# First layer's gate and up projections: seven block products in place of eight, for 19 of 22 tile pairs

## What is computed

```python
def swiglu(h, w_gate_up, w_down):
    gate, up = jnp.split(h @ w_gate_up, 2, axis=-1)
    return (jax.nn.silu(gate) * up) @ w_down
...
fx = rms_norm(x, g_ffn[i]) * (1.0 + sc2) + sh2
x = x + ga2 * swiglu(fx, w_gate_up[i], w_down[i])
if update_ctx:
    fc = rms_norm(ctx, g_ffn[i]) * (1.0 + csc2) + csh2
    ctx = ctx + cga2 * swiglu(fc, w_gate_up[i], w_down[i])
```

## Time and profile before

| what | us |
|---|---|
| median of 3 runs (1548.73 to 1551.69) | 1550.38 |
| the profiled execution's own time | 1552.32 |
| its span | 1550.5 |
| PE busy | 1377.4 |
| DVE busy | 699.2 |
| ACT busy | 512.4 |
| POOL busy | 66.2 |

### The profile page before, as it was taken

How to read it: one execution, slowest core, us unless ns; L and a number is a source line. 1 busy time by engine, 2 the same in 40 slices (tenths; PEclk the granted TensorE clock), 3 DMA queues, 4 the chain that set the end, 5 groups by cost and what they waited for, 6 DMA issues and landing times.

```text
span 1550.5 us, 24550 instructions
## 1 busy us (share of the span) xinstructions
PE 1377.4 (89%) x10275; PEld 1043.0 (67%) x10275; DVE 699.2 (45%) x1272; ACT 512.4 (33%) x946; POOL 66.2 (4%) x74
## 2 busy tenths in 40 slices
PE   6999999999999999999999999999987766766664
PEld 3765677887878787757999999899754334333332
DVE  4336546765645444675655657676521011010101
ACT  4426434222122223654444444555411101000001
POOL 1040020000000001111000000000000000000000
PEclk9999999999999999999999999999998878778888
DMA  8990325545844343616665459247899999999996
GB/s 339 411 296 1 136 82 211 200 152 186 299 167 169 114 162 107 207 38 248 212 208 187 130 183 303 84 138 273 360 425 426 425 427 425 426 426 426 426 426 265
DMA packets 159932, 392.40 MB, mean 253 GB/s; under 512 B 11573, under 2 KB 124745, under 8 KB 126026
## 3 DMA queue, kind: packets, MB, share of 16 engines
q1 hardware_dynamic: 159242, 389.34, 66.1%
q10 hardware_dynamic: 576, 1.44, 0.3%
HBM read 389.71 MB, written 1.05 MB: 252 GB/s over the span
## 4 chain that ended last, share of the span: by engine, by line
PE 65%; DMA 24%; DVE 5%; ACT 4%; issue 2%; SPq 0%; DVEq 0%; ACTq 0%
DMA R<-in_w_dram 22%; PE ps L1071 15%; PE ps L1072 15%; PE ps L1079 15%; PE ps L3121 3%; PE ps L1122 2%; PE ps L670 2%; PE ps L1116 2%; PE ps L1117 2%; DMA R<-in_w_ada_dram 2%; PE ps L1572 1%; PE ps L1549 1%; PE ps L3171 1%; PE ps L1517 1%; PE ps L1636 1%
## 5 line engine op out<-in xcount | busy, mean ns | idle before, releaser
L1039 DVE TENSOR_TENSOR WL<-R,WH 128x1024 fp32r<-128x1024 f32 (+1 forms) x201 | 225.2, 1137 | 165.0 <-ACT WH L1029 164.9
L3121 PE MATMUL ps<-R,XG 128*32 128x256 f32 x2048 | 172.8, 497 | 118.4 <-DMA R<-in_w_dram 112.3
L1071 PE MATMUL ps<-HH,WH 128*128 128x256 f32 (+2 forms) x872 | 273.0, 333 | 0.0
L1072 PE MATMUL ps<-HL,WH 128*128 128x256 f32 (+2 forms) x872 | 270.0, 331 | 0.0
L1029 ACT ACTIVATE WH<-R 128x1024 fp32r<-128x1024 f32 (+1 forms) x201 | 190.0, 961 | 140.5 <-PE ps L1079 105.5
L3121 PEld LDWEIGHTS ps<-R,XG 128*32 128x32 f32 x2048 | 87.6, 137 | 197.6 <-issue 179.9
L1071 PEld LDWEIGHTS ps<-HH,WH 128*128 128x128 f32 (+1 forms) x872 | 164.7, 189 | 25.5 <-issue 8.6
L1072 PEld LDWEIGHTS ps<-HL,WH 128*128 128x128 f32 (+1 forms) x872 | 164.1, 188 | 16.5
L1079 PE MATMUL ps<-HH,WL 128*128 128x256 f32 (+2 forms) x872 | 164.9, 331 | 0.0
L1071 PE MATMUL ps<-GH,WH 128*128 128x512 f32 (+1 forms) x480 | 154.5, 340 | 1.4 <-ACT WH L1029 1.4
L1072 PE MATMUL ps<-GL,WH 128*128 128x512 f32 (+1 forms) x480 | 153.4, 339 | 0.0
(11 more groups left out here) (509 smaller groups left out, 1729.1 us busy)
## 6 DMA issues: line engine op xcount, KB each, us to landing
R<-in_w_dram SPq DMA_DIRECT2D x192, 1024.0 KB, 26.5
R<-in_w_ada_dram SPq DMA_DIRECT2D x72, 1024.0 KB, 7.5
R<-in_w_gate_up_dram SPq DMA_DIRECT2D x40, 1024.0 KB, 6.4
R<-in_w_in_dram SPq DMA_DIRECT2D x20, 1024.0 KB, 7.7
R<-in_w_down_dram SPq DMA_DIRECT2D x16, 768.0 KB, 4.3
R<-in_w_down_dram SPq DMA_DIRECT2D x16, 640.0 KB, 4.2
R<-in_w_in_dram SPq DMA_DIRECT2D x8, 512.0 KB, 7.3
R<-in_w_out_dram SPq DMA_DIRECT2D x16, 256.0 KB, 8.3
```

Of the source, the lines that this page charges most:

```text
L1039: last = e.tensor_tensor(L, w, H.bitcast(F32), ALU.subtract)
L1071: e.matmul(b[0:n, 0:N], H[:, k, 0:n], xh(k, N), start=(begins and k == ks[0]), stop=False)
L1072: e.matmul(b[0:n, 0:N], H[:, k, 0:n], xl(k, N), start=False, stop=False)
L3121: mm = e.matmul(PS[4][32 * g:32 * g + 32, 0:256], x[:, 4 * hf + k, :], w[g // 2][:, k, 256 * (g % 2):256 * (g % 2) + 256], start=(hf == 0 ...
```

## The change

- Pairs m = 3 to 10 of half 0 and all 11 of half 1 (numbered p = 0 to 18) are no longer two tiles of 512 columns. The pair's weights are a 2 x 2 arrangement of blocks (gate or up, inputs 0 to 511 or 512 to 1023), the activations another (those inputs, `x` or `ctx`). Seven products of blocks (q = 0 to 6), each 12 matmuls of 256 columns, replace eight. The first three pairs of half 0 (`PLAIN`) stay.
- Three products take a weight block as it is loaded, four take sums of blocks (`SUMS`) which POOL makes: four instructions over 128 x 512 for a pair (`pool_seven`), and a fifth over 128 x 256 that adds two partial results of the pair before (`pool_up`). The activations' sums are made once, by DVE, behind the norm (`dve_sums_of_x`: 8 additions of 128 x 1024, four splits).
- ACT and DVE split each of the seven blocks (128 x 512) by itself, into four buffers in turn; the block that is split at step n is n + 4. DVE adds four partial results of 128 x 256 a pair, ACT copies two. The product with Silu is done for both streams by one DVE instruction.
- Five of the ring's ten slots are held from the start of half 0 to the end of half 1 (`kept`): three for the activations' sums, two for the weights' sums.
- Part 5 of the mixed-in sums has one vector in place of two. The mixed-in work follows product q = 2 of a pair, and the hooks of PE and ACT stand at pairs in place of tiles. One semaphore is renamed at the kernel's end.

Cut to what the prediction speaks of (`act_high_of_x`, `dve_low_of_x` split the activations' sums; `act_block` and `dve_block_low` for the first two blocks of a half are hung on the tile before it):

```diff
-VECTORS_OF = {5: (0, 1), 6: (2,), 7: (2,)}
+VECTORS_OF = {5: (0,), 6: (2,), 7: (2,)}
+PLAIN = 3
+PAIRS = [(half, m) for half in range(2) for m in range(11) if half or m >= PLAIN]
+BLOCKS = 7
...
+                    if i == 0 and (half, c // 128 + j) in PAIRS:
+                        pair_loads.append((gate, up, 128 * j, n))
+                        gate.used = up.used = (s_bl, blocks_split(BLOCKS * len(pair_loads)))
+                        continue
...
+                    if i == 0:
+                        kept = [ring.plan(None, hold=True, parts=0) for _ in range(5)]
...
+            if i == 0 and half:
+                for load in kept:
+                    load.used = (s_bm, BLOCKS * len(PAIRS))
+                    ring.held.discard(load.slot)
...
+    SUMS = [[at(f"SW{y}{q}", [128, 4, 128], F32, slot_at(kept[3 + y].slot) + 2 * KB * q) for q in range(4)] for y in range(2)]
...
+    UT = [TMP[7], TMP[6]]
...
+    def banks(p):
+        r = g00 % 4
+        A, B, C = ((PS[4], PS[5], PS[(r + 2) % 4]), (PS[(r + 3) % 4], PS[r], PS[(r + 1) % 4]))[p % 2]
+        return A[:, 0:256], C[:, 0:256], B[:, 0:256], C[:, 256:512]
...
+    def block_source(n):
+        p, q = divmod(n, BLOCKS)
+        gate, up, col, width = pair_loads[p]
+        if q in (0, 4, 6):
+            load = up if q == 6 else gate
+            k0 = 0 if q == 0 else 4
+            return fm(R[load.slot][:, 0:8 * width], 8)[:, k0:k0 + 4, col:col + 128], (d_ring[load.slot], load.landed)
+        x = {2: 0, 1: 1, 3: 2, 5: 3}[q]
+        return SUMS[p % 2][x][:, :, :], (s_sw, summed_weights(p, x))
+    def act_block(e, n):
...
+        if n >= 4:
+            e.wait_ge(s_bm, n - 3)
+        src, ready = block_source(n)
+        e.wait_ge(*ready)
+        e.activation(BH[n % 4][:, :, :], src, ACT.Copy).then_inc(s_bh, 1)
+    def act_product(e, p, x):
+        e.wait_ge(s_bm, BLOCKS * p + 2 * x + 1)
+        if p >= 2:
+            e.wait_ge(s_gu, number(p - 2) + 1)
+        elif p == 1:
+            e.wait_ge(s_bl, x_split(3))
+        e.activation(UT[p % 2][:, 256 * x:256 * x + 256], banks(p)[2 * x], ACT.Copy).then_inc(s_bh, 1)
+    def dve_block_low(e, n):
+        e.wait_ge(s_bh, high_of[n])
+        src, _ = block_source(n)
+        e.tensor_tensor(BL[n % 4][:, :, :], src, BH[n % 4][:, :, :].bitcast(F32), ALU.subtract).then_inc(s_bl, 1)
...
+    def pool_seven(e):
+        for p in range(len(PAIRS)):
+            gate, up, col, width = pair_loads[p]
+            s1, s2, s3, s4 = (t[:, :, :] for t in SUMS[p % 2])
+            if p == 0:
+                e.wait_ge(*kept[3].after.used)
+            elif p == 1:
+                e.wait_ge(s_bl, x_split(2))
+            else:
+                e.wait_ge(s_bl, blocks_split(BLOCKS * (p - 2) + 6))
+            for load in (gate, up):
+                e.wait_ge(d_ring[load.slot], load.landed)
+            g, u = (fm(R[load.slot][:, 0:8 * width], 8)[:, :, col:col + 128] for load in (gate, up))
+            e.tensor_tensor(s1, u[:, 0:4, :], u[:, 4:8, :], ALU.add).then_inc(s_sw, 1)
+            e.wait_ge(s_sw, summed_weights(p, 0))
+            e.tensor_tensor(s2, s1, g[:, 0:4, :], ALU.subtract).then_inc(s_sw, 1)
+            e.tensor_tensor(s3, g[:, 0:4, :], u[:, 0:4, :], ALU.subtract).then_inc(s_sw, 1)
+            e.wait_ge(s_sw, summed_weights(p, 1))
+            e.tensor_tensor(s4, g[:, 4:8, :], s2, ALU.subtract).then_inc(s_sw, 1)
+            if p and not goes_first(p - 1):
+                pool_up(e, p - 1)
+            if goes_first(p):
+                pool_up(e, p)
+    def pool_up(e, p):
+        ut = UT[p % 2]
+        e.wait_ge(s_cmb, 8 + 4 * p + 2)
+        if p >= 3:
+            e.wait_ge(s_gu, number(p - 3) + 1)
+        e.tensor_tensor(TMP[3 + p % 3][:, 256:512], ut[:, 0:256], ut[:, 256:512], ALU.add).then_inc(s_sw, 1)
...
+    def dve_sums_of_x(e):
+        def whole(k0, c0):
+            return HH[:, k0:k0 + 4, c0:c0 + 256].bitcast(F32), HL[:, k0:k0 + 4, c0:c0 + 256].bitcast(F32)
+        e.wait_ge(*kept[4].after.used)
+        e.wait_ge(s_hl, made(1, 7, 1))
+        for out, k0, c0 in ((F12, 0, 256), (F11, 0, 0), (F22, 4, 256), (F21, 4, 0)):
+            e.tensor_tensor(out[:, :, :], *whole(k0, c0), ALU.add).then_inc(s_cmb, 1)
...
+        for x in range(3):
+            dve_low_of_x(e, x)
...
+    def pe_seven(e, half, after):
+        for p in half_pairs(half):
+            a, b, c, d = banks(p)
+            if p >= 2:
+                e.wait_ge(s_gu, number(p - 2) + 1)
+            if p in half_pairs(half)[0:2]:
+                r, first = g00 % 4, p == half_pairs(half)[0]
+                for x in ((2,) if first else (3, 4, 5)):
+                    t = g00 + x if half == 0 else first_of["down", 0, 0] + x + 2
+                    e.wait_ge(*tiles[t].out)
+            for q, acc in enumerate((a, b, c, d, a, c, d)):
+                n = BLOCKS * p + q
+                xh, xl = x_part(q, False), x_part(q, True)
+                if p == 0 and q in X_READY:
+                    e.wait_ge(s_bl, x_split(X_READY[q] - 1))
+                if q == 3:
+                    e.wait_ge(s_cmb, 8 + 4 * p + 1)
+                elif q == 5:
+                    e.wait_ge(s_cmb, 8 + 4 * p + 2)
+                e.wait_ge(s_bh, high_of[n])
+                for k in range(4):
+                    e.matmul(acc, BH[n % 4][:, k, :], xh(k), start=(q < 4 and k == 0), stop=False, skip_group_check=True)
+                    e.matmul(acc, BH[n % 4][:, k, :], xl(k), start=False, stop=False, skip_group_check=True)
+                e.wait_ge(s_bl, blocks_split(n + 1))
+                for k in range(4):
+                    last = e.matmul(acc, BL[n % 4][:, k, :], xh(k), start=False, stop=(k == 3), skip_group_check=True)
+                last.then_inc(s_bm, 1)
+            after(PAIRS[p][1])
+    def act_rounded(e, p):
+        m, g = PAIRS[p][1], number(p)
+        e.wait_ge(s_gu, g + 1)
+        e.activation(GH[:, m, :], TMP[m % 3][:, :], ACT.Copy).then_inc(s_fh, 1)
+    def act_seven(e, half, then, hook):
+        blocks = half_blocks(half)
+        for x in (2, 3):
+            act_block(e, blocks[x])
+            if half == 0 and x == 2:
+                act_high_of_x(e, 3)
+        for n in blocks:
+            p, q = divmod(n, BLOCKS)
+            m, g = PAIRS[p][1], number(p)
+            T = TMP[m % 3]
+            if q == 0:
+                hook(m)
+            if n + 4 in blocks:
+                act_block(e, n + 4)
+            if q in (0, 2):
+                act_product(e, p, q // 2)
+            if q == 0 and n != blocks[0]:
+                act_rounded(e, p - 1)
+            if n == blocks[-2]:
+                act_split(e, then)
+            if q == 4:
+                e.wait_ge(s_bm, n + 1)
+                e.wait_ge(s_fl, g - 2)
+                e.activation(T[:, 0:256], banks(p)[0], ACT.Silu)
+            elif q == 5:
+                e.wait_ge(s_cmb, 8 + 4 * p + 3)
+                e.activation(T[:, 256:512], T[:, 256:512], ACT.Silu).then_inc(s_silu, 1)
+        act_rounded(e, blocks[-1] // BLOCKS)
...
+    def dve_seven(e, half, then, hook, weigh):
+        blocks = half_blocks(half)
+        for x in (2, 3):
+            dve_block_low(e, blocks[x])
+            if half == 0 and x == 2:
+                dve_low_of_x(e, 3)
+        for n in blocks:
+            p, q = divmod(n, BLOCKS)
+            m, g = PAIRS[p][1], number(p)
+            T, V, ut = TMP[m % 3], TMP[3 + p % 3], UT[p % 2]
+            a, b, c, d = banks(p)
+            if q == 0:
+                hook(m)
+                if n != blocks[0]:
+                    dve_rest(e, p - 1)
+            elif q == 1:
+                e.wait_ge(s_bm, n + 1)
+                dve_pair_sum(e, p, 0, ut[:, 0:256], b)
+            elif q == 3:
+                e.wait_ge(s_bm, n + 1)
+                dve_pair_sum(e, p, 1, ut[:, 256:512], d)
+            elif q == 5:
+                e.wait_ge(s_bm, n + 1)
+                e.wait_ge(s_cmb, 8 + 4 * p + 1)
+                e.wait_ge(s_fl, g - 2)
+                e.tensor_tensor(T[:, 256:512], c, ut[:, 0:256], ALU.add).then_inc(s_cmb, 1)
+            elif q == 6:
+                e.wait_ge(s_bm, n + 1)
+                if p >= 3:
+                    e.wait_ge(s_gu, number(p - 3) + 1)
+                e.tensor_tensor(V[:, 0:256], d, ut[:, 0:256], ALU.add).then_inc(s_cmb, 1)
+                e.wait_ge(s_cmb, 8 + 4 * p + 4)
+                e.wait_ge(s_sw, added(p))
+                e.wait_ge(s_silu, g + 1)
+                e.tensor_tensor(T[:, :], T[:, :], V[:, :], ALU.mult).then_inc(s_gu, 1)
+            if n + 4 in blocks:
+                dve_block_low(e, n + 4)
+            if q == 2:
+                weigh(m)
+        dve_rest(e, blocks[-1] // BLOCKS)
+        dve_split(e, then)
+    def dve_pair_sum(e, p, x, ut, product):
+        e.wait_ge(s_bh, high_of["p", p, x])
+        e.tensor_tensor(ut, product, ut, ALU.add).then_inc(s_cmb, 1)
...
+            if i or half == 0:
```

(34 more changed lines are left out.)

158 lines of the change are left out of this document (128 added, 30 removed).

## The result

| kernel | median us | ratio to before (95%) |
|---|---|---|
| before | 1551.04 (1548.73 to 1552.04, 4 runs) | |
| after | 1683.72 (1683.27 to 1684.77, 4 runs) | 1.0853 (1.0839 to 1.0866) |

The change costs 133 us. The forecast was 1642, with a range up to 1680: the sign and the mechanism of the two halves came as forecast, the size did not, and the stage between the halves was missed. In the profiled executions the span goes from 1550.5 to 1681.5, 131 us more.

What follows compares the result with a forecast made beforehand. The prediction took PE alone to bound the changed stage. Its terms summed to 95.6 us, less 4 for shared effects: 92 on the profiled 1552.3, giving 1644 and a median of 1642, range 1600 to 1680.

Steps and rivals of the forecast that it cites:

- seven dear boundaries: Group boundaries in both halves: late loads, sums and splits in series lose 10.3 us each, 72 in all.
- Rival B: In the halves, POOL and DVE do not hinder each other, ring boundaries remain: cycle 28 to 29, total 1612; chance 0.10.
- D: In the halves, loads do not matter and only POOL and DVE exclusion binds: +24 us, total 1583; chance 0.08.
- The landing of both loads: At a group boundary, gate and up loads land 6.4 us after DVE's split releases their slots.
- The rest of a boundary: After landing: POOL's sums 6.4 us, DVE's product, splits and first partial sum 6.6, the stretch from product 3 13.3.
- the load k = 3: In half 1, this weighting waits a whole landing for a slot freed by the split just ahead: 3 us.
- The start at 5.5: Before the first pair: 2 us from POOL's sums during the norm, 3.5 from ACT's delayed split of tile 5.
- The eighth boundary: Into half 0's last pair: loads of half the size and no sums behind them, 4 us.
- half 1's first pair: At half 1's start, it meets its own sums, the next pair's and part 6's last weighting on POOL: 8 us.
- the small rest: Deductions: 0.9 us for part 5's dropped vector on PE, 4 for overlap with short pairs at half 1's end.
- Rival E: At boundaries, same mechanism but POOL's sums take 2.15 us each and DVE waits longer: 44 more, total 1686; chance 0.13.
- number 3: Sign expected in the profile: DVE's product waits for POOL's short sum, 5 us and more, seven times.

Runs made afterwards that it cites:

- e9: Changed kernel with all five block sums of a pair on DVE instead of POOL, nothing left out: 1635.18 us, ratio 1.0537 to the kernel before.
- e2: Changed kernel with POOL writing constants in place of its five sums per pair: two pairs take 27.4 us, against 36.4 in the changed kernel.
- e1: Changed kernel without gate and up loads after each half's first group, whose weights are reused: two pairs take 26.9 us, against 36.4.
- e6: Changed kernel with SP issuing a group's two weighting loads only after its up load has landed: 1684.34 us, ratio 1.085.
- e8: Changed kernel without part 6's loads and weightings for k from 1 on: first down stage 63.1 us, against 72.7 in the changed kernel.
- e4: Changed kernel with POOL making the previous pair's short sum ahead of the next group's four sums at group boundaries: 1680.51 us, ratio 1.0824.
- e12: Changed kernel without loads and weightings of parts 5 and 7 for k from 1 on: two pairs take 23.9 us, against 36.4.

## Why the prediction was wrong

Right: the one-to-one passing of the stage's loss to the end (131 us in all, 126 of them by the end of half 1), products of 1.44 us on PE, mutual exclusion of POOL and DVE, gate and up released by DVE's splits, seven dear boundaries, PE's waits ahead of products 1 and 3 (4.0 and 6.1 us forecast as 1 to 4 and 5 to 8). The rule of the Trainium skill that the prediction leaned on (SBUF — State Buffer, Who interferes with whom) holds over the whole stage: DVE's product and splits beside POOL's sums took 1.70 and 1.76 us, a split 0.69 in e9, where POOL is quiet, and 0.68 to 0.69 in e2, where POOL only writes. Rival B's cycle of 28 to 29 us was close to the 27.4 that e2 shows for its mechanism, and D's 24 us of exclusion to the 30 of e1 (which also has the length of POOL's sums in it).

Wrong was the size, 92 in place of 131, and these are the terms:

- **The landing of both loads, 6.4**, is 8.0. I took the median over single loads for the time of a pair issued together (e6). 1.6 us at each of seven boundaries.
- **The rest of a boundary.** With the landing a boundary was forecast to lose 10.3 us (a cycle of 32.7) and loses 14.0 (36.4); 2.1 of the 3.7 are not the landing. POOL's five came to 6.7 for 6.4. The product, the three that follow it and the first partial sum took 7.2 for 6.6: the product, which I had at 0.6, itself ran into POOL's first sum for the next pair (1.70). The stretch from product 3 on took 14.5 for 13.3, with TensorE's granted clock at 0.50 over 4 us after the wait:

```profile
334.90:341.00 6.10, 0.17 (x2) 0.00 (x0) 6.10 (x6) 1.94 (x4) 5.22 (x4) 0.67 0.00 0
341.00:345.00 4.00, 3.87 (x18) 3.87 (x19) 4.00 (x6) 0.63 (x1) 0.05 (x1) 0.50 0.01 4
```

  This is the 1.2 GHz level. The seven cycles took 35.3, 36.4, 35.6, 35.7, 38.1, 36.2 and 36.5 us, 97 more than 7 x 22.4; forecast were 72, with 3 for the load k = 3 and 4 for the clock 79.
- **The down stages at nothing.** I gave them no term at all. In the kernel after, ACT and PE in the first one:

```profile
462.47 0.84 ACT L1057 ACTIVATE WH<-R 128x768 fp32r<-128x768 f32 x1 [13.82 <-DMA R<-in_w_down_dram]
...
466.60 2.10 ACT L1057 ACTIVATE WH<-R 128x640 fp32r<-128x640 f32 x3 [3.29 <-DMA R<-in_w_down_dram]
```

```profile
467.48 0.77 PE L1387 MATMUL ps<-GH,WH 128*128 128x512 f32 x1 [4.40 <-ACT WH L1057]
```

  The five kept slots are kept through this stage too, so part 6's loads and the down weights share what the pairs share, with the same result: 10.6 us there. e8 shows that part 6's weightings are the rival for the slots; that it is the five kept slots that make them one is inferred, from the kernel before, where both fit without a gap. Asking for each stage what the five slots take from it would have found it. Behind half 1 it is another 5.3 us: 2.7 of PE's wait for the last pair's product, and 2.6 in the kernel's last 25 us, where behind the last load that PE waits for there are 9.0 us of its work left in place of 2.8. I know no cause for these 2.6.
- **The start at 5.5** was 9.6. I followed ACT's copies to tile 5's split, which was right in kind (done at 263.0, forecast 260.6), but not one step further in ACT's queue:

```profile
261.02 1.06 ACT L1241 ACTIVATE TH<-F 128x1024 fp32r<-128x1024 f32 x1 [0.20 <-DVE F L1227]
261.99 1.04 ACT L1057 ACTIVATE WH<-R 128x1024 fp32r<-128x1024 f32 x1
263.04 1.28 ACT L2174 ACT_TABLE_LOAD   x1
264.34 0.60 ACT L2174 ACTIVATE TMP<-ps 128x512 f32<-128x512 f32 x1
```

```profile
264.99 0.79 PE L1387 MATMUL ps<-HH,WH 128*128 128x512 f32 x1 [5.79 <-ACT TMP L2174]
```

  Behind the split stand a table load and tile 0's Silu, which frees the PSUM bank that PE needs. The 9.6 are 2 us by which the four tiles ahead end later (forecast 2), 5.8 of this wait (forecast 3.5), and 1.8 for the two tiles behind it, which no term had: TensorE goes on at a granted clock of 0.50 and 0.56 until 269 us.

18 (boundaries) + 10.6 + 5.3 + 4.1 is 38.0. The eighth boundary (5.4 for 4) and half 1's first pair (9.2 for 8) bring it to 40.6, and the small rest, -4.9 in the forecast, came to -6.2: the 19 pairs of before took 218.5 us with their mixed-in work and not 19 x 11.2 = 212.8, and the last two pairs of after 21.9 in place of 22.4. That gives the 39 that were missing; the largest are the boundaries (18) and the first down stage (10.6). Rival E named 1686 and came within 3 us, but not by its mechanism: it wanted POOL's sums at 2.15 each, and they were 1.26 to 1.74; that its number was near is luck. Of the forecast's signs, number 3 was misplaced: DVE's long wait stood at a split that needs POOL's second sum (5.05), not at the product (0.36). The forecast had DVE stand in the product "with all its later splits and sums behind it"; e4 shows that taking the short sum out of the way gives the stage nothing.

Open stays what part of the 48 us of e9 is exclusion and what is POOL's slower sum (1.26 against 0.69), since e9 takes both away, and why the loads are late again at the start of e12's half 1. No run held fewer than five slots, so that the slots are the cause of the late loads is inferred from `Ring.plan` and from e8 and e12, where taking the weightings out of the slots brought the loads in time.

## What to carry to other kernels

A saving on the bound engine of 10% (10.08 for 11.20 us) has to be set against what its buffers take away: here five of ten load slots, and with them gone loads that were hidden became 8 us of bare landing every second pair. Two costs that are bearable apart (38 and 30 us) can be worth 98 together when a late load puts them in series, so price them in the order of the boundary, and price every stage through which the buffers are held. A landing time is taken from the last load of a group issued together, not from the median over all.
